# Attention of a hybrid diffusion block on one core: head projections in blocks of four heads, q's norm inside the exponential, unsplit scores, and 24 modulation tiles moved from TensorE to VectorE

## The reference, cut to what matters

```python
mod_x = split((silu(c) @ ada_w[i] + ada_b[i]), 6)      # and mod_c from silu(c_ctx)
h = rms_norm(x, norm_mix) * (1 + mod[1]) + mod[0]
cq, ckv, kr = split(h @ w_in, [512, 768])
q  = (rms_norm(cq, q_norm) @ w_uq)       # 16 heads, 64 plain + 32 rotary columns
kv = (rms_norm(ckv, kv_norm) @ w_ukv)    # 16 heads, 64 key + 64 value columns
rotary on the 32 columns of q and on kr (latent tokens only); k = [k_nope, kr]
s = q k^T / sqrt(96);  p = softmax(s);  out = (p v) @ w_o
# latent queries see all 512 keys, context queries the 256 context keys
```

## Time and profile before

| what | value |
|---|---|
| three runs | 1305.38, 1305.78, 1312.1 us; median 1305.78 |
| the profiled execution: its own time / its span | 1306.43 / 1304.6 us |
| mean TensorE clock granted | 0.967 of full |
| busy: PE, DVE, ACT, POOL | 91%, 64%, 45%, 18% |
| heads: first row maximum of head 0 / of head 15 | 112.21 / 283.88 us |
| first matmul of the output projection | 294.61 us |
| silu of the c rows (128x2048) on ACT, and its table load | 1.91 and 1.28 us, near 295 us |

### The profile page before, as it was taken

The page is one execution under the profiler, slowest core; times in us unless marked ns, Lnnn a source line. Parts: engine busy times, 40 slices in busy tenths (PEclk is TensorE's granted clock), DMA queues, the critical chain, the costliest instruction groups (busy, mean ns, idle before and its releaser), DMA issues.

```text
span 1304.6 us, 21131 instructions
## 1 busy us (share of the span) xinstructions
PE 1193.1 (91%) x7484; PEld 996.7 (76%) x7484; DVE 836.5 (64%) x1269; ACT 587.9 (45%) x999; POOL 234.9 (18%) x205
## 2 busy tenths in 40 slices
PE   5797999979899999999999879998988778999997
PEld 3575777767888888887888867888844578999996
DVE  0756667653578777775665687877478665655554
ACT  3545666664352222222222466455533254666542
POOL 0102443431200000000111200001278622000011
PEclk9899999999999999999999999999989889999998
DMA  9312333221056555554444123223500025466662
GB/s 377 124 45 95 128 127 127 97 86 65 1 199 220 193 193 193 189 190 156 154 153 141 49 80 106 81 83 124 181 1 1 0 67 192 130 194 193 184 188 79
DMA packets 50472, 169.12 MB, mean 130 GB/s; under 512 B 5488, under 2 KB 8816, under 8 KB 50160
## 3 DMA queue, kind: packets, MB, share of 16 engines
q1 hardware_dynamic: 50416, 168.37, 38.3%
HBM read 167.30 MB, written 1.05 MB: 129 GB/s over the span
## 4 chain that ended last, share of the span: by engine, by line
PE 71%; DVE 9%; issue 9%; POOL 4%; ACT 3%; DMA 2%; SPq 1%; DVEq 0%; POOLq 0%; ACTq 0%
PE bank L1500 22%; PE bank L1502 21%; PE bank L1501 21%; DVE scratch L1419 1%; PE bank L1898 1%; PE bank L1910 1%; DMA raw<-in_w_in 1%; POOL scratch L447 1%; POOL scratch L445 1%; PE bank L1920 1%; DVE w_lo L969 1%; DVE scratch L1304 1%; POOL q_lo L453 1%; ACT w_hi L572 1%; PE bank L1929 1%
## 5 line engine op out<-in xcount | busy, mean ns | idle before, releaser
L969 DVE TENSOR_TENSOR w_lo<-raw,w_hi 128x1024 fp32r<-128x1024 f32 (+1 forms) x242 | 282.3, 1174 | 179.9 <-ACT w_hi L572 179.7
L572 ACT ACTIVATE w_hi<-raw 128x1024 fp32r<-128x1024 f32 (+1 forms) x242 | 234.1, 976 | 267.8 <-PE bank L1502 242.7
L1500 PE MATMUL bank<-ffn_h_lo,w_hi 128*128 128x256 f32 (+1 forms) x736 | 243.9, 331 | 9.1 <-DVE ffn_h_lo L1006 4.9
L1501 PE MATMUL bank<-ffn_h_hi,w_hi 128*128 128x256 f32 (+1 forms) x736 | 243.1, 330 | 0.0
L1502 PE MATMUL bank<-ffn_h_hi,w_lo 128*128 128x256 f32 (+1 forms) x736 | 243.0, 330 | 0.0
L1500 PEld LDWEIGHTS bank<-ffn_h_lo,w_hi 128*128 128x128 f32 x736 | 140.0, 190 | 24.6 <-issue 5.2
L1501 PEld LDWEIGHTS bank<-ffn_h_hi,w_hi 128*128 128x128 f32 x736 | 140.0, 190 | 14.5
L1502 PEld LDWEIGHTS bank<-ffn_h_hi,w_lo 128*128 128x128 f32 x736 | 139.8, 190 | 14.5
L414 POOL TENSOR_TENSOR scratch<-scratch 128x512 f32<-128x512 f32 (+1 forms) x24 | 37.0, 1541 | 599.8 <-ACT scratch L581 599.8
L1500 PE MATMUL bank<-ffn_hidden_lo,w_hi 128*128 128x256 f32 (+1 forms) x374 | 123.0, 329 | 5.8 <-DVE ffn_hidden_lo L1263 5.8
L1500 PE MATMUL bank<-ssd_h_lo,w_hi 128*128 128x256 f32 (+2 forms) x360 | 120.1, 334 | 8.6 <-DVE w_lo L969 5.0
(11 more groups left out here) (245 smaller groups left out, 2222.1 us busy)
## 6 DMA issues: line engine op xcount, KB each, us to landing
raw<-in_w SPq DMA_DIRECT2D x120, 512.0 KB, 4.4
scratch<-in_vec_w SPq DMA_DIRECT2D x56, 512.0 KB, 3.4
cq<-in_ada_w SPq DMA_DIRECT2D x24, 512.0 KB, 4.4
raw<-in_w_xbc SPq DMA_DIRECT2D x24, 512.0 KB, 3.4
ada_start<-in_ada_w SPq DMA_DIRECT2D x8, 1024.0 KB, 17.4
raw<-in_w_z SPq DMA_DIRECT2D x16, 512.0 KB, 3.6
raw<-in_w_so SPq DMA_DIRECT2D x16, 512.0 KB, 4.3
raw<-in_w SPq DMA_DIRECT2D x16, 384.0 KB, 4.0
```

Of the source, the lines that this page charges most:

```text
L572: A(wh[s % RING][:, 0:c], raw[s % RING][:, 0:c], ACT.Copy).then_inc(w_hi, 1)
L969: V.tensor_tensor(wl[s % RING][:, 0:c], raw[s % RING][:, 0:c], wh[s % RING][:, 0:c].bitcast(f32), SUB).then_inc(w_lo, 1)
L1500: mm(o, lh, rl, start=first, stop=False)
L1501: mm(o, lh, rh, start=False, stop=False)
```

## The change

The names: `HEAD_BLOCKS` is a list of 16 weight tiles of 128x512. For each group g of four heads there are K (keys of four heads in two halves), A and B (plain q columns of two heads each) and C (rotary columns of four heads). The order is K0 A0 B0 C0, then A B C K of groups 1, 2, 3. Five blocks are made before head 0; `head(i)` makes block i+5 (so heads 1, 5, 9 make a C, heads 2, 6, 10 a K, and heads 11 to 15 none). q and k are held in plain single precision for six and four heads, and `scores` is one single-precision matmul each instead of three split ones; the low parts of q and k go. q's rms is no longer multiplied in: cq is rounded with q's gain right behind its projection, and 1/rms enters as the scale of the exponential (`q_scale`) and a factor of the negative maxima (`q_neg`). The rotation's swap of halves is a matmul with a permutation (`swap`), and `rotate` on VectorE does four heads at once. `ada_two` is gone from the heads: 24 modulation tiles are now `matvec_mla` on VectorE, 8 before the heads, 12 in heads 0, 2, 3, 4, 6, 7, 8, 10 to 14, and 4 in the output projection. silu of the c rows moves ahead of `t = 0`. Values are read from `v` without a copy. All 16 heads are written out, with no hardware loop. The table of constants grows by 128 columns.

```diff
+HEAD_BLOCKS = [("K", 0), ("A", 0), ("B", 0), ("C", 0)] + [(kind, g) for g in range(1, 4) for kind in "ABCK"]
+ROPE_STEPS = [b - 5 for b, (kind, g) in enumerate(HEAD_BLOCKS) if kind == "C" and g]
+VEC_STEPS = [i for i in range(15) if i not in ROPE_STEPS]
...
                 load(IN + t, IN + t, 1024, one("w_in", t))
...
+            vec(0, vec_mla[:, 0, :])
...
+            at = VEC_HEADS
+            for i in range(HEADS):
+                b = i + 8
+                if b < 16:
+                    load(HP + b, HP + b, 512, one("w_heads", b))
+                elif i - 8 < 4:
+                    t = i - 8
+                    load(WO + t, WO + t, 1024, one("w_o", t))
+                if i in VEC_STEPS:
+                    vec(at, vec_mla[:, at % 2, :])
+                    at += 1
...
+            act.wait_ge(crow_in, 16)
+            A(crow[:, :, :], crow[:, :, :], ACT.Silu).then_inc(crow_silu, 1)
...
+                    k = t - 3
+                    square(2, k, bank[t % 2][:, :])
+                    A(cnh[:, KKV + k, :], bank[t % 2][:, :], ACT.Copy, scale=par[:, PAR["q_norm"] + k:PAR["q_norm"] + k + 1]).then_inc(proj_out, 1)
...
+                if kind == "K":
+                    for half in range(2):
+                        if half:
+                            act.wait_ge(w_used, HP + b + 1)
+                        else:
+                            act.wait_ge(k_mm, g + 1)
+                        if g:
+                            act.wait_ge(s_mm, 3 * h)
+                        for u in range(2):
+                            A(kf[0:64, 2 * half + u, :], banks[half][64 * u:64 * u + 64, :], ACT.Copy).then_inc(k_out, 1)
+                elif kind == "C":
+                    act.wait_ge(w_used, HP + b + 1)
+                    if g:
+                        act.wait_ge(rope_part, 2 * g)
+                    A(qr[:, :], banks[0][:, :], ACT.Copy).then_inc(q_raw, 1)
+                    act.wait_ge(q_raw, g + 1)
+                    if h >= 4:
+                        act.wait_ge(s_mm, 3 * (h - 2))
+                    for u in range(4):
+                        A(qf[64:96, q_slot(h + u), 0:CTX], qr[32 * u:32 * u + 32, 0:CTX], ACT.Copy).then_inc(q_ctx, 1)
+                else:
...
+                    for u in range(2):
+                        A(qf[0:64, q_slot(h + u), :], banks[0][64 * u:64 * u + 64, :], ACT.Copy).then_inc(q_nope, 1)
+                if b + 4 < 16 + 4:
+                    hi(HP + b + 4, HP + b + 4)
...
+                    A(P[:, p, :], bank[p][:, :], ACT.Exp, bias=nm[:, p:p + 1], scale=q_scale[:, 2 + p:3 + p],
...
+            def head(i):
+
+                for p in range(3):
+                    pt_split(i, p)
+                if i < 15:
+                    for p in range(3):
+                        exps(i + 1, p)
+                if i + 5 < 16:
+                    project_out(i + 5, (bank[7], bank[7]))
                 act.wait_ge(o_mm, i + 1)
...
+                if t >= 3:
+                    k = t - 3
+                    dve.wait_ge(proj_out, t + 1)
+                    V.scalar_tensor_tensor(cnl[:, KKV + k, :], bank[t % 2][:, :], par[:, PAR["q_norm"] + k:PAR["q_norm"] + k + 1],
+                                           cnh[:, KKV + k, :].bitcast(f32), MUL, SUB).then_inc(cq_lo, 1)
...
-            norm(2, lambda k, c0, c1: cq[:, KKV + k, c0:c1], KQ, whole, lambda k, m: par[:, PAR["q_norm"] + k:PAR["q_norm"] + k + 1],
-                 lambda k, c0, c1: cnh[:, KKV + k, c0:c1], lambda k, c0, c1: cnl[:, KKV + k, c0:c1], None)
+                if t == 0:
+                    dve.wait_ge(crow_silu, 1)
+                if t < 6:
+                    matvec_mla(t)
...
+            matvec_mla(7)
...
+            def rotate(g, b):
+
+                h = 4 * g
+                dve.wait_ge(q_raw, g + 1)
+                if g:
+                    dve.wait_ge(q_rope, h)
+                V.tensor_tensor(rope_c[:, :], qr[:, CTX:TOK], tabv("cos", LAT), MUL).then_inc(rope_part, 1)
+                dve.wait_ge(q_perm, g + 1)
+                V.tensor_tensor(rope_s[:, :], b[:, 0:LAT], tabv("sin", LAT), MUL).then_inc(rope_part, 1)
+                dve.wait_ge(rope_part, 2 * g + 2)
+                if h >= 4:
+                    dve.wait_ge(s_mm, 3 * (h - 2))
+                for u in range(4):
+                    r = slice(32 * u, 32 * u + 32)
+                    V.tensor_tensor(qf[64:96, q_slot(h + u), CTX:TOK], rope_c[r, :], rope_s[r, :], ADD).then_inc(q_rope, 1)
...
-                V.tensor_scalar(nm[:, c], mx[:, c], -(float(QKD) ** -0.5), None, MUL).then_inc(nmax, 1)
+                V.tensor_tensor(nm[:, c], mx[:, c], q_neg[:, 2 + p:3 + p] if p < 2 else q_neg[:, 0:2], MUL).then_inc(nmax, 1)
...
-            def head(i, j, u):
-                n, s = HL + 2 * i, HL + 2 * (i if isinstance(i, int) else u)
-                more = not isinstance(i, int) or i < 15
-                if more:
-                    project(i + 1, n, s)
...
-                if more:
+            def head(i, v):
...
                     maxes(i + 1, 2)
                     inverse(i + 1, 1)
                     inverse(i + 1, 2)
-                if u and (not isinstance(i, int) or i < 12):
-                    ada_out(4 + j, 0, 4 + j)
+                if i + 5 < 16 + 4:
+                    if i + 5 < 16:
+                        lo(HP + i + 5 + 4, HP + i + 5 + 4)
+                    if i in ROPE_STEPS:
+                        rotate(HEAD_BLOCKS[i + 5][1], bank[7])
+                if v is not None:
+                    matvec_mla(v)
                 for r in range(2):
...
+            for b in range(2, 5):
+                lo(HP + b + 2, HP + b + 2)
+            rotate(0, bank[2])
+            for b in range(5, 7):
+                lo(HP + b + 2, HP + b + 2)
...
+                if m < 4:
+                    matvec_mla(VEC_OUT + m)
+            bias(0, 24, 40, 24)
+            gains(1, 0, 4, "norm_ffn", vec_bias, 2, 2)
...
+                if t >= 5:
+                    pe.wait_ge(cq_lo, t - 4)
...
+                    w = slice(256 * half + 128 * k, 256 * half + 128 * k + 128)
+                    last = three(o[:, :], wh[sl][:, w], wl[sl][:, w], cnh[:, k, :], cnl[:, k, :], k == 0, k == KKV - 1)
+                last.then_inc(w_used if half else k_mm, 1)
...
+            def swap(b, o):
+
+                g = HEAD_BLOCKS[b][1]
+                pe.wait_ge(q_raw, g + 1)
+                mm(o[:, 0:LAT], tabv("swap"), qr[:, CTX:TOK], start=True, stop=True).then_inc(q_perm, 1)
...
-            def values(i, u):
+            def values(i):
...
                 for p in range(3):
                     transpose_probs(i, p)
-                ada = not isinstance(i, int) or i < 12
-                if ada:
-                    ada_two(ADA0 + 4 * j + 2 * u, u, ada_mla)
...
-
-            project(0, HP, HP)
-            pe.wait_ge(kr_lo, 1)
+                if i < 15:
+                    for p in range(3):
+                        scores(i + 1, p)
+                if kind:
+                    bank7_free(b)
+                if kind == "K":
+                    k_tile(b, 0, bank[7])
+                elif kind:
+                    q_tile(b, bank[7])
+                values(i)
+                if kind == "K":
+                    pe.wait_ge(k_out, 4 * g + 2)
+                    k_tile(b, 1, bank[7])
+                elif kind == "C":
+                    swap(b, bank[7])
+
+            pe.wait_ge(proj_out, 7)
+            pe.wait_ge(cq_lo, KQ)
+            k_tile(0, 0, bank[0])
+            k_tile(0, 1, bank[1])
+            q_tile(1, bank[7])
+            pe.wait_ge(v_out, 8)
+            q_tile(2, bank[5])
+            q_tile(3, bank[2])
+            pe.wait_ge(q_nope, 2)
+            q_tile(4, bank[7])
+            swap(3, bank[2])
+            pe.wait_ge(kr_cp, 3)
+            pe.wait_ge(k_out, 4)
+            pe.wait_ge(q_nope, 4)
             for p in range(3):
                 scores(0, p)
-            head(0, 0, 0)
-            head(1, 0, 1)
-            with pe.Fori(1, 6) as j:
-                head(2 * j, j, 0)
-                head(2 * j + 1, j, 1)
-            head(12, 6, 0)
-            head(13, 6, 1)
-            head(14, 7, 0)
-            head(15, 7, 1)
+            for i in range(HEADS):
+                head(i)
```

More of the change, by code:

```diff
@@ L91, in block_cols @@
     cols = [1024] * NBLK
[L92 to L94 removed]
+    for n in range(HP, HP + 16):
+        cols[n] = 512
     cols[DT] = 512
```

380 lines of the change are left out of this document (163 added, 217 removed).

## The result

The changed kernel takes 1327.71 us (median of 4 runs, 1325.31 to 1329.82) against 1306.21 for the kernel before (4 runs, 1305.38 to 1312.1): ratio 1.0154, 95% interval 1.012 to 1.0189. It is slower, by 21.5 us between the medians (20 by the ratio). I had forecast 1303.5 with a range of 1290 to 1314, so the time lies outside it. The profiled execution took 1329.82 us, span 1328.0.

The account below looks back on a forecast made before the run. It took VectorE's in-order stream, not TensorE, to set the heads' pace after the change. Heads -14.7, start +6.3, end +1.7 and clock +4.2 summed to -2.5 us, giving 1303.5 us, range 1290 to 1314.

Parts of the forecast that it names:

- the start: Stretch up to head 1's first row maximum, with modulation products between weight splits: forecast 6.3 us later.
- heads 1 to 15: From head 1's first maximum to head 15's: forecast 146.0 us against 160.7 before, a gain of 14.7.
- the end: Head 15's values wait for head 14's low part behind its products: forecast 1.7 us more.
- the clock: TensorE at half clock after longer waits: bounds 0 and 8.6 us, half taken, +4.2.
- the wait ahead of `t = 6`: In the start, TensorE waits for the low part of cq until 85.3: forecast +3.5 us.
- 1.1 us for the last heads: Heads 11 to 13: added time for VectorE's products running beside GpSimd's last scaling, 1.1 us a head.
- the 8.85: Forecast us from head 0's first maximum to head 1's: 6.1 for maxima and inverses, 2.75 for scaling, transposes and one score.
- D = 4.28: In each head, first row maximum to end of last inverse: 4.28 us, taken as unchanged from before.
- the plain and C periods: Forecast between first maxima: 9.5 us with block A or B, 10.9 with C; 10.5 and 11.9 in heads 7 to 10.
- The K periods: Heads making a K block, whose second half waits for ScalarE's copies: forecast 12.1, 12.1 and 13.1 us.
- The three terms that I had priced: Half-clock losses: K block's second half 3.6 us, last transposes and first score 2.7, start 2.3; together 8.6.
- The third rival: Slower, by a low TensorE clock in every head: 11 us more, 1314 us; chance 0.17.

Follow-up runs that it names:

- e2: Kernel before with an unused one-column tile behind the gains, moving every stage's tiles 32 bytes on: 1316.63 us, ratio 1.0068.
- e12: Changed kernel with its one-column epsilon tile made 64 columns wide, giving later tiles their places of the kernel before: 1320.26 us, ratio 1.0102 against that kernel.
- e5: e1 with modulation products 3 to 5 moved behind the loop over the first seven weight blocks: 1317.63 us, ratio 1.0069 against the kernel before.
- e9: e3 with the second half of each K block in bank 2 instead of bank 7: 1304.89 us, ratio 0.9973 against the kernel before.
- e8: e1 with an unused 256-column TensorE product ahead of each of a head's three waits for scaled probabilities: 1313.42 us, ratio 1.0051 against the kernel before.
- e4: e1 with the heads' twelve modulation products run over 8 of 1024 columns, leaving out most of their sum: 1297.12 us, ratio 0.9917 against the kernel before.
- e1: Changed kernel with its one-column epsilon tile made 16 columns wide, so later tiles start at a multiple of 128 bytes: 1320.94 us, ratio 1.009 against the kernel before.
- e3: e1 with the heads' modulation products moved ahead of the split that waits for ScalarE: 1310.85 us, ratio 1.0023 against the kernel before.
- e13: Kernel before with an unused tile of 256 bytes behind the gains, moving everything 256 bytes on: 1307.22 us, ratio 0.9999.
- e6: e3 and e5 together, with the second layer's tiles moved 64 bytes on: 1302.16 us, ratio 0.9962 against the kernel before.
- e11: e6 plus the edits of e8 and e9, with the second layer's tiles at 64 beyond a multiple of 256 bytes: 1285.62 us, ratio 0.9828 against the kernel before.

## Why the prediction was wrong

The profiled execution was to take 1303.9 and took 1329.8, 25.9 more. At the output projection's first matmul it was 17.0 late (7.7 from the start, 12.5 from heads 1 to 15, 1.1 from the end, less the 4.2 that were set aside for the clock), and behind it 8.9 came on top. By the steps of the prediction:

- **Left out: the place of the tiles, +9.2.** The sum ended at the output projection and took everything behind it as unchanged. Its instructions were; a four-byte tile moved their operands (e2, e12). The term was put at nothing without a reason.
- **The start, +6.3 at head 1's maximum, came out at +14.0** (137.15 against 123.19). Step by step: the wait ahead of `t = 6` ended at 86.99 and not 85.3, because contention with GpSimd, which I had priced at 1.1 us for the last heads, also met two VectorE instructions here. The tile then ran in part at the low clock and took 8.3 us, against 5.6 for its 24 matmuls at 0.2333. Head 0's maximum was 5.7 late; e5, with a wait of 2.81 us and the full clock, put it at 119.93, near the 120.6 of the prediction. From head 0 to head 1 the 8.85 became 10.82, TensorE's granted clock being 0.52 from 130 to 136 us.
- **Heads 1 to 15, -14.7, came out at -2.2** (158.5). 4 of the 12.5 us are the exponential's factor: I took D = 4.28 from before with the words that nothing in the change shortens it, and didn't ask what lengthens it. An instruction with one more operand column was a new form. Beyond that, the plain and C periods whose clock was 1.00 were right within about 0.2 (9.93 and 11.4). The K periods were 14.0, 13.1 and 15.0 for 12.1, 12.1 and 13.1. Their copies waited 3.02, 2.06 and 3.02 us for 1.6: the shared bank put that wait on the chain (e9), as the prediction had it, and what came on top in heads 2 and 10 was mostly the low clock. The period from head 1 to 2 was 11.81 at a clock of 0.86, and heads 12 to 14 lost 1.7 (e8 gives them back).
- **The clock, +4.2 with bounds of 0 and 8.6.** The mechanism was right, its size was not. By my estimate it cost 2.7 in `t = 6`, up to 3.9 in the K heads, 1.7 in heads 12 to 14, 1.7 from head 0 to 1 and 1.9 from head 1 to 2 (against 9.93 at 1.00; the others are the excess over the forecast without the factor's 0.28): 12 us, which are part of the items above. The three terms that I had priced came to 8.3, near the bound of 8.6 and about twice what I took; the 3.6 from head 0 to head 2 I had not priced.
- **The end, +1.7, came out at +2.8** (13.51 us from head 15's first maximum to the output projection, against 10.73). The wait itself was right: values of head 15 began 304.94 - 300.88 = 4.06 us behind D, forecast 4.2. But head 15's D was 5.24 and not 4.28: the factor, and a second maximum that waited 0.82 us for TensorE's score at the low clock.
- **Structure:** right. VectorE's stream set the pace, with the products behind the split, so TensorE was not the bound (e4). The third rival, a low clock in every head, isn't what happened: A and B heads from 174 to 205 us ran at 1.00. The Trainium skill (TensorE: Matmul & The Clock Gate, HAM oscillation) names the pattern of a wait between bursts; here low stretches lay in the first heads, the K heads, one C head (0.86 from 240.23 to 252.58) and the last heads. TensorE waited 3.83 to 3.86 us in each K head, and 0.5 to 0.7 us in the A and B heads at 1.00.
- **Given back:** 3.6 us between the output projection and the second layer, which I hadn't counted. They are spread over that stretch, in e12 it gives back 2.1, and the cause stays open.

What stays open: what makes the gap go by the place, why it has two levels at some places, and whether K heads would run at full clock with longer filling.

## What to carry to other kernels

Before pricing what a change does, list what it moves in SBUF: a new tile ahead of others shifts every operand behind it, and TensorE's distance between matmuls went by that, 4 to 6% for 256 columns, in parts of the program that the diff doesn't touch. Compare matmul counts in equal stretches of an untouched stage first. In an in-order stream, put work that waits for nothing ahead of the instruction that waits: the same products cost 18.7 us behind ScalarE's split and 7.8 ahead of it (heads' sums of e1 and e3 against e4). Price every instruction that gets a new operand, and give a low clock a price wherever a wait grows, not only where the trace of before had one.

## What the runs showed of the hardware

A three-pass fp32 matmul of 256 columns was issued every 0.1133, 0.1178, 0.1183 or 0.1200 us, one of 512 every 0.2267 or 0.2333, by where the tiles of the stage start, at a granted clock of 1.00 throughout; in the state-space part one of 512 took 0.2285 to 0.2333. Tiles 256 bytes on gave the same gaps (e13), tiles 128 bytes on did not (0.2290 in e6, 0.2331 in e11). The Trainium skill (SBUF — State Buffer, Operand start alignment) treats alignment as a question of legality and says that its runs timed nothing; these did. At 64 beyond a multiple of 128 the gap of 256 columns held one of two values, 0.1133 or 0.1178, through each unbroken row of products. A scale taken from a column instead of a number lengthened a ScalarE exponential by 90 ns, at 512 columns and at 256 alike. A VectorE product of 1024 columns took 2.28 us beside a GpSimd instruction and 1.22 alone, and the GpSimd instruction 2.33, where the same one in the kernel before took 1.30. And unused TensorE products ahead of the waits, three a head, went with a granted clock of 1.00 for 0.83 in the last three heads and made them 2.45 us faster.
